# The surplus tile of a mixture of experts: its expert is placed at the head of the last pack and its tile is computed between the last experts

## The reference

```python
# 4 groups of 8 experts = 32; a token takes the best group, and the two best experts in it
combine = (g_onehot[:, :, None] * (g_weight[:, None] * e_w)[:, None, :])
for g in range(N_GROUPS):
    h = silu(einsum('nd,edf->nef', xt, w_gate[g])) * einsum('nd,edf->nef', xt, w_up[g])
    out = out + einsum('nef,efd->nd', h * combine[:, g, :, None], w_down[g])
```

## Time and profile before

| | |
|---|---|
| median of 3 runs | 1179.64 us (1178.2 to 1191.04) |
| the profiled execution | 1180.25 us |
| its span, first to last instruction | 1178.5 us |
| TensorE busy (matmul) | 918.3 us, 78% of the span |
| VectorE, ScalarE, GpSimd busy | 502.8, 371.4, 203.1 us |
| moved by DMA | 299.83 MB, mean 254 GB/s |
| chain that ended last | PE 58%, DMA 25%, DVE 7%, ACT 5% |

### The profile page before, as it was taken

The page is one execution under the profiler, slowest core; times in us unless marked ns, Lnnn a source line. Parts: engine busy times, 40 slices in busy tenths (PEclk is TensorE's granted clock), DMA queues, the critical chain, the costliest instruction groups (busy, mean ns, idle before and its releaser), DMA issues.

```text
span 1178.5 us, 18327 instructions
## 1 busy us (share of the span) xinstructions
PE 918.3 (78%) x7868; PEld 738.5 (63%) x7869; DVE 502.8 (43%) x817; ACT 371.4 (32%) x510; POOL 203.1 (17%) x76
## 2 busy tenths in 40 slices
PE   4987477756666666665666599998999998999996
PEld 4987475433333333333434299668999997988985
DVE  4435535312020112121111549998983566453541
ACT  4453311111010111111112434446655444434330
POOL 1021400000000000000001668702239830000000
PEclk8998688888787878787878799999999999999998
DMA  9850553999999999999997245314457643454510
GB/s 356 266 204 1 200 228 130 407 423 420 422 422 419 424 421 423 422 421 424 419 422 286 68 134 188 119 51 154 160 177 244 216 143 132 154 204 167 200 71 36
DMA packets 94894, 299.83 MB, mean 254 GB/s; under 512 B 9165, under 2 KB 45565, under 8 KB 86653
## 3 DMA queue, kind: packets, MB, share of 16 engines
q1 hardware_dynamic: 94125, 297.95, 65.4%
q0 software_dynamic: 576, 1.18, 0.4%
q10 hardware_dynamic: 144, 0.00, 0.0%
HBM read 298.07 MB, written 1.05 MB: 254 GB/s over the span
## 4 chain that ended last, share of the span: by engine, by line
PE 58%; DMA 25%; DVE 7%; ACT 5%; issue 2%; SPq 2%; DVEq 0%; ACTq 0%
DMA mem<-in_w_up 22%; PE PS L1588 13%; PE PS L1589 13%; PE PS L1590 13%; PE PS L1743 8%; PE PS L1757 3%; PE PS L1905 2%; DMA mem<-in_w 1%; DMA mem<-in_w_in 1%; PE PS L1730 1%; PE PS L1581 1%; ACT mem L648 1%; PE PS L1770 1%; DVE m_rest L1514 1%; DVE HN L1100 1%
## 5 line engine op out<-in xcount | busy, mean ns | idle before, releaser
L1743 PE MATMUL PS<-mem 128*32 128x256 f32 x2112 | 163.8, 479 | 119.6 <-DMA mem<-in_w_up 115.0
L1590 PE MATMUL PS<-HT_hi,ring_rest 128*128 128x256 f32 x768 | 218.4, 284 | 0.0
L1743 PEld LDWEIGHTS PS<-mem 128*32 128x32 f32 x2112 | 88.2, 137 | 196.5 <-issue 175.3
L588 POOL TENSOR_TENSOR ring_rest<-mem,z_hi 128x2048 fp32r<-128x2048 f32 x21 | 97.4, 4642 | 621.9 <-ACT z_hi L791 537.9
L1590 PEld LDWEIGHTS PS<-HT_hi,ring_rest 128*128 128x128 f32 x768 | 148.4, 193 | 0.0
L1588 PE MATMUL PS<-HT_hi,z_hi 128*128 128x256 f32 x448 | 129.0, 288 | 9.7 <-ACT mem L840 5.8
L1589 PE MATMUL PS<-HT_rest,z_hi 128*128 128x256 f32 x448 | 128.2, 286 | 0.0
L1532 DVE TENSOR_TENSOR ring_rest<-mem,mlp_hi 128x4096 fp32r<-128x4096 f32 x16 | 70.6, 4425 | 81.5 <-ACT mlp_hi L938 81.5
L1209 DVE TENSOR_TENSOR mem<-mem,PS 128x128 f32<-128x128 f32 x33 | 9.5, 287 | 222.0 <-ACT mem L764 221.9
L1588 PEld LDWEIGHTS PS<-HT_hi,z_hi 128*128 128x128 f32 x448 | 87.6, 195 | 11.5 <-ACT mem L840 6.2
L1418 DVE SCALAR_TENSOR_TENSOR PS<-mem,CAW,PS 128x256 f32<-128x256 f32 x232 | 91.2, 484 | 0.0
(11 more groups left out here) (326 smaller groups left out, 1837.8 us busy)
## 6 DMA issues: line engine op xcount, KB each, us to landing
mem<-in_w_gate SPq DMA_DIRECT2D x32, 2048.0 KB, 14.3
mem<-in_w_up SPq DMA_DIRECT2D x32, 2048.0 KB, 18.8
mem<-in_w_down SPq DMA_DIRECT2D x32, 2048.0 KB, 11.7
mem<-in_w SPq DMA_DIRECT2D x16, 2048.0 KB, 7.9
mem<-in_w_in SPq DMA_DIRECT2D x28, 1024.0 KB, 5.3
mem<-in_w_in SPq DMA_DIRECT2D x5, 2048.0 KB, 19.7
mem<-in_w_b_out SPq DMA_DIRECT2D x4, 1536.0 KB, 9.5
mem<-in_w_out SPq DMA_DIRECT2D x2, 2048.0 KB, 14.6
```

The source lines that it names most:

```text
L588: nc.gpsimd.tensor_tensor(z_rest(n), z_raw(n), z_hi(n).bitcast(F32), ALU.subtract).then_inc(z_rest_ready, 1)
L1590: ins = nc.tensor.matmul(dst, s_rest, m_hi, start=False, stop=stop and n == len(terms) - 1, skip_group_check=True)
L1743: ins = nc.tensor.matmul(PS[SLOTS * j:SLOTS * (j + 1), B_GATE + i % 2, 0:2 * F_STRIP].rearrange("p (w n) -> p w n", w=2), XG[:, k, SLOTS * ...
```

## The change

- The last over-full expert, if its place is 4 or more, now goes to place 28 (`OVER_AT`), the first of the last pack.
- The expert in place 28 is loaded to the third slots, 29 to ODD, 30 to EVEN, 31 to ODD. The loop over pairs of loads ends with expert 27; `place` follows.
- If the first extra tile's expert stands in place 28, SyncE only signals `over_loaded`; if not ("elsewhere"), it waits for expert 28's down product and loads that expert's three matrices into the third slots.
- The extra tile has its own buffers, cut from HT (`over_X`, `over_hid`, `over_Y` and others) and its own semaphores, and takes the gather bank for its products. TensorE runs its gather, gate and up between expert 28 and expert 29, its down after 29's gate and up, its combine after 29's down; expert 30 begins after its last add.
- The last pack of ScalarE is written out; the splits of the first two z halves come after it. Further extra tiles follow in a loop behind the pack, as before. The semaphores `rms_ready` and `rows` are one each with counts.

The diff, cut to its core:

```diff
-            with sp.Fori(2, EXPERTS // 2) as pair:
+            with sp.Fori(2, OVER_AT // 2) as pair:
...
+            def placed(p):
+                return sp.value_load(order_i[0:1, p:p + 1], min_val=0, max_val=EXPERTS - 1)
+
+            w = placed(OVER_AT)
+            load_gate_up(w, third)
+            load_down(w, *third[2])
+            w = placed(OVER_AT + 1)
+            sp.wait_ge(gu_done, OVER_AT)
+            load_gate_up(w, second)
+            sp.wait_ge(down_done, OVER_AT)
+            load_down(w, *second[2])
+            w = placed(OVER_AT + 2)
+            load_gate_up(w, first)
+            load_down(w, *first[2])
+
+
+            def over_expert(j):
+                e = sp.value_load(extra_i[0:1, 1, bass.ds(j, 1)], min_val=0, max_val=EXPERTS - 1)
+                return sp.value_load(order_i[0:1, bass.ds(e, 1)], min_val=0, max_val=EXPERTS - 1)
+
+            def load_over(w):
+                load_expert(w, [p for p, _ in third[0:2]], [over_loaded, over_loaded])
+                load_down(w, third[2][0], over_loaded)
+
+            n_extra = sp.value_load(extra_i[0:1, 0, 0:1], min_val=0, max_val=EXTRA_MAX)
+            with sp.If(n_extra > 0):
+                w = over_expert(0)
+                again = sp.value_load(extra_i[0:1, 2, 0:1], min_val=0, max_val=1)
+                with sp.If(again < 1):
+                    sp.sem_inc(over_loaded, 3 * 16)
+                with sp.If(again > 0):
+                    sp.wait_ge(down_done, OVER_AT + 1)
+                    load_over(w)
+
+            w = placed(OVER_AT + 3)
+            sp.wait_ge(gu_done, OVER_AT + 2)
+            load_gate_up(w, second)
+            sp.wait_ge(down_done, OVER_AT + 2)
+            load_down(w, *second[2])
             sp.wait_ge(down_done, EXPERTS - 1)
             for n in range(RAW):
                 load_z(n)
...
-            def extra_weights(j):
-                e = sp.value_load(extra_i[0:1, 1, bass.ds(j, 1)], min_val=0, max_val=EXPERTS - 1)
-                w = sp.value_load(order_i[0:1, bass.ds(e, 1)], min_val=0, max_val=EXPERTS - 1)
-                again = sp.value_load(extra_i[0:1, 4, bass.ds(j, 1)], min_val=0, max_val=1)
-                with sp.If(again < 1):
-                    for part in range(3):
-                        sp.sem_inc(extra_loaded[part], 16)
-                with sp.If(again > 0):
-                    sp.wait_ge(down_done, j + EXPERTS)
-                    load_expert(w, [slot[s] for s in ODD[0:2]], extra_loaded[0:2])
-                    load_down(w, slot[ODD[2]], extra_loaded[2])
-
-            n_extra = sp.value_load(extra_i[0:1, 0, 0:1], min_val=0, max_val=EXTRA_MAX)
-            with sp.If(n_extra > 0):
-                extra_weights(0)
...
+            def over_tile(j):
+                act.wait_ge(over_x_ready, j + 1)
+                nc.scalar.activation(over_CT, PS[0:SLOTS, B_GATHER, T:2 * T], ACT.Copy).then_inc(over_ct, 1)
+                act.wait_ge(over_gu, j + 1)
+                nc.scalar.activation(over_silu, PS[:, B_GATHER, 0:P], ACT.Silu).then_inc(over_gated, 1)
+                act.wait_ge(over_turned, j + 1)
+                nc.scalar.activation(over_hidT, PS[:, B_TURN, 0:P], ACT.Copy).then_inc(over_hidT_ready, 1)
+                act.wait_ge(over_down_done, j + 1)
+                for n in range(2):
+                    ins = nc.scalar.activation(over_Y[:, D_STRIP * n:D_STRIP * (n + 1)],
+                                               PS[SLOTS * n:SLOTS * (n + 1), B_GATHER, 0:D_STRIP], ACT.Copy)
+                ins.then_inc(over_y, 1)
+
+            act.wait_ge(extra_ready, 1)
+            n_extra = act.value_load(extra_i[0:1, 0, 0:1], min_val=0, max_val=EXTRA_MAX)
+            turn_combine(PACKS - 1)
+            for i in range(PACK):
+                gate(OVER_AT + i, i)
+                hidden_turned(OVER_AT + i, i)
+                collect(OVER_AT + i, i)
+                if i == 0:
+                    with act.If(n_extra > 0):
+                        over_tile(0)
+
             split_half(0)
             split_half(1)
...
-                spare = extra_f[:, 5, 1:2]
-                link(nc.vector.tensor_scalar(spare, last_row, float(PACK), float(EXPERTS), ALU.is_lt, ALU.mult))
-                link(nc.vector.tensor_tensor(last_row, last_row, spare, ALU.add))
-                link(nc.vector.tensor_scalar(last_row, last_row, float(EXPERTS - 1), None, ALU.min))
+                stay = extra_f[:, 5, 1:2]
+                link(nc.vector.tensor_scalar(stay, last_row, float(PACK), float(OVER_AT), ALU.is_lt, ALU.mult))
+                link(nc.vector.tensor_tensor(last_row, last_row, stay, ALU.max))
...
+                elsewhere = extra_f[:, 2, 0:16]
+                link(nc.vector.tensor_scalar(elsewhere, extra_row[:, 1, :], float(OVER_AT), None, ALU.not_equal))
+                nc.vector.tensor_copy(extra_i[:, 2, :], elsewhere)
+                nc.vector.tensor_copy(extra_i[:, 0:2, :], extra_row[:, 0:2, :]).then_inc(extra_ready, 1)
...
+            def over_hidden(j):
+                dve.wait_ge(over_gath, j + 1)
+                nc.vector.tensor_tensor(over_X, PS[:, B_GATHER, 0:KC * SLOTS].rearrange("p (k s) -> p k s", k=KC),
+                                        gains[:, G_FFN, :].unsqueeze(2).broadcast_to((P, KC, SLOTS)), ALU.mult).then_inc(over_x_ready, 1)
+                dve.wait_ge(over_gated, j + 1)
+                nc.vector.tensor_tensor(over_hid, over_silu, PS[:, B_GATHER, P:2 * P], ALU.mult).then_inc(over_hid_ready, 1)
+
+            def over_outputs(j):
+                dve.wait_ge(over_down_done, j + 1)
+                for n in range(2, 4):
+                    ins = nc.vector.tensor_copy(over_Y[:, D_STRIP * n:D_STRIP * (n + 1)],
+                                                PS[SLOTS * n:SLOTS * (n + 1), B_GATHER, 0:D_STRIP])
+                ins.then_inc(over_y, 1)
+                for n in range(4):
+                    half, tt = slice((n // 2) * BLOCK, (n // 2 + 1) * BLOCK), n % 2
+                    dve.wait_ge(over_comb, 4 * j + (n + 1))
+                    nc.vector.tensor_tensor(X[:, tt, half], X[:, tt, half], PS[:, B_COMB + n % 2, :], ALU.add).then_inc(over_added, 1)
+                dve.wait_ge(over_added, 4 * j + 4)
+                dve.sem_inc(over_finished, 1)
+
+            with dve.If(n_extra > 0):
+                over_select(0)
             for i in range(PACK):
-                hidden(EXPERTS - PACK + i, i)
-                if i == 2:
-                    with dve.If(n_extra > 0):
-                        take_gathered(PACKS, SLOTS)
-                collect(EXPERTS - PACK + i, i)
+                hidden(OVER_AT + i, i)
                 if i == 1:
                     with dve.If(n_extra > 0):
-                        extra_select(0)
+                        over_outputs(0)
+                collect(OVER_AT + i, i)
+                if i == 0:
+                    with dve.If(n_extra > 0):
+                        over_hidden(0)
             add_pack(PACKS - 1)
-            with dve.If(n_extra > 0):
-                extra_outputs(0)
+            dve.wait_ge(comb_free, 4 * PACKS + 2)
...
+                if isinstance(pack, int) and pack == PACKS - 1 and i % 2 == 0:
+                    if i == 0:
+                        return third_at + part * SLOT_FLOATS, (third_loaded, 16 * 6)
+                    return s * SLOT_FLOATS, (loaded[s], 32 * pack + 16)
...
+            def over_gate_up(j):
+                pe.wait_ge(over_sel, j + 1)
+                if isinstance(j, int):
+                    pe.wait_ge(xg_ready, 2 * PACKS)
+                    pe.wait_ge(ct_ready, PACKS)
+                else:
+                    pe.wait_ge(over_y, 2 * j)
+                for k in range(KC):
+                    for tt in range(TT):
+                        ins = nc.tensor.matmul(PS[:, B_GATHER, k * SLOTS:(k + 1) * SLOTS], HN[:, tt, k, :], sel[:, tt, 0:SLOTS],
+                                               start=tt == 0, stop=tt == TT - 1)
+                for tt in range(TT):
+                    ins = nc.tensor.transpose(PS[0:SLOTS, B_GATHER, T + tt * P:T + (tt + 1) * P], selw[:, tt, 0:SLOTS], ident[:, :])
+                ins.then_inc(over_gath, 1)
+                pe.wait_ge(over_loaded, 3 * 16 * j + 3 * 16)
+                pe.wait_ge(over_x_ready, j + 1)
+                pe.wait_ge(over_ct, j + 1)
+                gate_up(third_at, B_GATHER, over_X, over_gu)
+
+            def over_down(j):
+                pe.wait_ge(over_hid_ready, j + 1)
+                nc.tensor.transpose(PS[:, B_TURN, 0:P], over_hid, ident[:, :]).then_inc(over_turned, 1)
+                pe.wait_ge(over_hidT_ready, j + 1)
+                down(third_at + 2 * SLOT_FLOATS, B_GATHER, over_hidT, over_down_done)
+
+            def over_combine(j):
+                pe.wait_ge(over_y, 2 * j + 2)
+                pe.wait_ge(comb_free, 4 * (PACKS - 1 if isinstance(j, int) else PACKS) + 2)
+                for n in range(4):
+                    half, tt = n // 2, n % 2
```

(25 more changed lines are left out.)

161 lines of the change are left out of this document (67 added, 94 removed).

## The result

The changed kernel took 1205.86 us (median of 4 runs, 1203.58 to 1209.37), the kernel before, on the same chip, 1181.52 (median of 4, 1178.2 to 1191.04). The ratio is 1.0162, interval 1.0129 to 1.0196: slower by 1.6%. The forecast of 1191.0 had the sign and the reload as its cause, but 1205.86 lies outside its range of 1187 to 1199.

The account below looks back on a forecast made before the run. It took full DMA queues plus a TensorE tail to bound the expert stage. Chain 10.1, late ScalarE 0.4 and joins 0.4 made 10.9; with the profiled 1180.25 that is 1191.15, so 1191 us, range 1187 to 1199.

Parts of the forecast that it names:

- The reload: Last pack: SyncE loads expert 2 a second time, 99 tiles, not 96, landing at 633.8, with TensorE idle over 30 us.
- The z loads: SyncE behind the experts: these loads wait for expert 30's down product, 661.75; before they waited from 637.55.
- the splits: ScalarE after expert 31: the first splits of z halves start at 667.3 and 671.5, 5.5 and 9.7 after first issue.
- the table load: ScalarE behind the splits: 1.28 us, ending at 674.7 against a last add at 674.3, so 0.4 late.
- One of the prediction's own signs of being wrong: Listed profile signs: 96 loads with last add near 641, a gap before expert 31, clock 0.5 after 645, a GpSimd wait.
- 29's Silu to end of its down: Chain after the reload lands: ScalarE copies half the tile's output first, Silu at 646.7, then 1.34 and 1.95, to 650.0.
- tile's combine and join: Chain behind 29's down: combine to last add 4.6 us plus 0.15 for the signal, to 654.8, with nothing beside it on TensorE.
- expert 30: Chain behind the tile's combine: 3.66 + 1.34 + 1.95 us, to 661.75.
- The cold chain: Rival: TensorE's clock low along the chain after the reload, 14.5 us at most, +10 giving 1201; chance 0.08.
- the third rest: First z round: TensorE wants this GpSimd result at 703, GpSimd has it at 699, a cover of 4 us.
- The weights stay: Rival: no reload in the last pack, last add at 641.4, time 1159.5 us; chance 0.08.
- joins: New branches and value loads between the parts, five on TensorE: bounds 0 and 1.5 us, taken as 0.4.

Follow-up runs that it names:

- e1: Changed kernel with the reload taken out, the tile using expert 28's weights (not the reference's tile): 1167.34 to 1184.66 us in three runs, ratio 0.9897.
- e2: Changed kernel reloading only expert 2's gate matrix, up and down staying expert 28's (not the reference's tile): 1204.81 us, one run.
- e5: Changed kernel with the loads of the kernel before: third slots keep expert 2, nothing is loaded again: 1173.67 us, ratio 0.9899.
- e12: Changed kernel unchanged, profiled a second time: 1202.01 us, 1.012 of its set's median of before.
- e10: Changed kernel, reload kept, with GpSimd's second rest moved behind its 12 table DMAs: 1202.14 us, ratio 1.0116.
- e3: Changed kernel with GpSimd's first two rests held until VectorE's two products with the gain are done: 1211.85 us, ratio 1.0182.
- e9: Changed kernel with filler products on TensorE, 118 in the reload's wait and more in the last pack's gaps: 1224.67 us, ratio 1.0311.
- e11: e8 with the fillers of e9 in the last pack's gaps, 4 in place of the 118: 1172.28 us, ratio 0.9874.
- e8: e7 with the tile's combine moved behind expert 30's gate and up products: 1170.87 us, ratio 0.9865.
- e7: e5 with GpSimd's second rest moved behind its 12 table DMAs: 1175.01 us, ratio 0.9911.
- e4: Kernel before, with GpSimd's two rests held until the last adds: 1193.65 us, ratio 1.0046.
- e6: Changed kernel, reload kept, with the tile's gather, products and combine moved between experts 30 and 31: 1188.86 us, ratio 1.004.

## Why the prediction went wrong, and where it was right

**The reload: right.** 99 tiles, landing at 632.5 for 633.8 forecast, a gap of 32.34 us, 0 GB/s from 634 to 642, no wait before expert 31's product, three more loads landing ahead of the tile's product. e1, e2 and e5 show it as the cause of the loss. The z loads at 664.46 (661.75 forecast), the splits 672.13 + 3.71 and the table load that ends at 677.14, 0.2 behind the last add (0.4 forecast), and GpSimd ready with its DMAs at 698.4 (694.6 forecast, with a last add 2.6 earlier) without a wait of TensorE in the first z round: right too. No table load follows the branch, as forecast. One of the prediction's own signs of being wrong did occur: a granted clock of 0.50 after 645.

**The first step that failed is in the chain: the products behind the first one were put down as warm.** The terms, from the landing to the last add, in us (each term ends where the next one begins, at the start or the end of a product; the last column is the second execution of the same code):

```
                                     forecast   after    e12
tile's gate and up                      5.8      5.1     4.9
29's gate and up                        3.66     3.6     3.6
tile's transpose, copy, down            2.65     2.6     2.6
29's Silu to end of its down            4.1      5.9     4.2
tile's combine and join                 4.75     5.5     5.0
expert 30                               6.95     9.3     8.6
expert 31                               6.95     6.9     6.9
copy, combine, last add                 5.6      5.6     5.6
sum                                    40.5     44.4    41.4
```

In the profile of after three terms are longer, 29's down (+1.8), the combine (+0.8) and expert 30 (+2.3), each with products at a clock of 0.50; the others are 1.0 shorter together, which leaves +3.9. In e12 it leaves +0.9. Two more profiles have the same code up to the last add: e10 with 44.1 (+3.6) and e3 with 46.8 (+6.3). The cold chain stood among the rivals with 0.08, its deciding point ("when gaps of 1.3 to 2 us let the clock fall") named, and set aside by the earlier trace rows, where the clock was full at 657 after two gaps of 1 us. That row has no tile's combine in front of it. It does have the pack's combine, four products of the same size but from 128 rows in place of 32, and 1.02 us idle behind them; and in the profiles of before and after each of the seven earlier combines of this kind is directly followed by a product at 3.66. So the row was true and said nothing of the new combine. Two things were mixed in the rival. A clock of 0.50 at or behind the tile's combine came in all twelve profiles of kernels that have it (the next gate and up product 5.17 to 6.56 in nine, fillers at 0.95 in e9 and e11, the down product at 3.64 in e8) and should have been in the sum, at 1.5 to 2.9. The fall at 29's down came in some (after, e1, e2, e3, e7, e8: 2.50 to 3.62) and not in others (e5, e10, e12: 1.93), with the same work ahead of it, and belonged in the range. The rival's price, +10, was too high: the truth, +0.9 to +6.3, lay between the two cases. The Trainium skill (TensorE: Matmul & The Clock Gate, What's actually happening) has throttled as the default and activity as what releases it; the runs agree as far as e9 goes, where activity in the gaps kept the clock up to the combine. For its fall there, with TensorE busy for most of the time, only these rows speak. What in the combine brings it about, its 32 rows, its waits for adds or the wait behind it, wasn't separated, and that cause stays open.

**The second step that failed isn't in the sum at all: who works beside whom in the norm.** I moved ScalarE's splits and GpSimd's rests some 29 us later, priced GpSimd as a queue ("works off two rests (9.03), the memsets and its 12 DMAs"), and asked only whether the third rest would be late for TensorE. That was answered rightly, with a cover of 4 us. But the first rests thereby left a stretch where VectorE had little to do and came to lie over VectorE's products of the norm. Cost: +4.9, shown from three sides. e4 makes it in the kernel before (+7.8 of norm, +5.6 of time); e7 and e10 take 4.1 of it away (19.8 to 15.7 in both; the 0.8 left goes with VectorE's products at 3.21 for 2.36 and the idle time ahead of them, 0.74 for 0.16); e3 moves it onto operations of two columns, which speaks for an exclusive hold and against shared bandwidth. The Trainium skill (SBUF — State Buffer, Who interferes with whom) states it: a VectorE instruction with two SBUF inputs contends with a GpSimd instruction that reads SBUF; it calls the contention an exclusive lock, and says of VectorE's 2-port modes that the one that comes second is blocked for the whole instruction of the other. The runs agree: 4.42 us for a product of 0.16 until GpSimd's instruction ends, while VectorE's last adds, with one input in PSUM, stay at 0.69 beside the same rests. Whether the scaling's 4.93 in e3, with one input in SBUF and beside memsets, is the same thing was not tested.

**The rest.** Of the +24.5, -2.1 lie ahead of the last pack and +6.9 behind the z phase. e12 shows that the latter is no fixed cost of the code. But the other three timed runs of the changed kernel were as long as the profiled one (1203.58 to 1209.37), so on that chip it may well be what the shift usually makes of the alignment; that was not profiled, and stays open. So it can't be said which part of the miss would come again: in e12's set the changed kernel was 14.0 us over the median of before (one run), in its own 24.3. In the eleven other kernels the stretch behind the z phase was 496.8 to 504.9, with no relation to the edit. The forecast took it as unchanged, and its range held nothing for it.

In sum, 24.5 - 10.9 = 13.6 us were missing: 2.6 at the last add (the 3.9 of the chain, less 1.3 for the earlier landing), 4.5 in the norm beyond what was forecast, 6.9 behind the z phase, less 0.4 of joins placed outside these. The first two make 1191.15 + 7.1 = 1198.3, still in the range; only the third, which may be chance, takes it out. "The weights stay", tried as e5, has 53.4 for the last pack, where that rival's working gave 641.4 - 591.3 = 50.1; the 3.3 are again the cold product behind the combine (2.9 of it).

## What to carry to other kernels

Before weights are left in a slot until the end, find out by the inputs which expert's they are: a reload at the end of a full stream costs its tiles (4.97 us of stream each here) plus everything that stands behind its wait, and moving the waiting work behind other work gets most of it back (e6). When a change shifts GpSimd's work in time, lay its new interval over VectorE's timeline and price every VectorE instruction with two SBUF inputs that it covers at the end of GpSimd's instruction, tiny ones too; holding GpSimd back by a wait may only move the collision (e3), moving it behind GpSimd's memsets and DMA issues shortens the norm by 4 us (e7, e10), though no gain in time was clear of the noise. And when short, dependent products are laid between long ones on TensorE, put at least one product behind them at the low clock.

## What the runs showed of the hardware that was not expected

- A VectorE product of 128x2 elements took 4.42 us in place of 0.16, beside a GpSimd operation of 4.5 us (e3).
- TensorE's granted clock was 0.50 behind the tile's combine (four products of 128x512 from 32 rows, x8 in the trace, with waits for adds between) or right after it in twelve of twelve profiles, and e9's fillers up to it didn't prevent it; behind the pack's combines in the profiles of before and after, four products of that size from 128 rows, the next products ran at the full clock (3.66, and 1.93 after 1.02 us idle). The tile's combine itself took 3.88 where the clock held through it (e5) and 7.19 where it didn't (e3).
- A DMA issue on SyncE took 10.09 us with some six tiles of 2 MB queued, and so held everything behind it in SyncE's order (e6).
- Two executions of the same code differ by 7.5 us behind the z phase. 1.6 of them are there before the first, and 6.1 by the last, of four VectorE operations of 0.7 us that may meet GpSimd's rests.
